# Hybrid decoder trunk on one core: down matrices of the experts issued by ScalarE

## What is computed

```python
def run_chunk(args):
    xc, e = args
    return (jax.nn.silu(xc @ w_gate[e]) * (xc @ w_up[e])) @ w_down[e]

ys = lax.map(run_chunk, (xs, chunk_exp)).reshape(n_rows, d)
out = jax.ops.segment_sum(ys * row_w[:, None].astype(ys.dtype), row_tok, num_segments=n_tok)
```

## Time and profile before

| | us |
|---|---|
| median of 3 runs | 1696.39 (1695.54 to 1699.03) |
| the profiled execution | 1697.77 |
| its span in the trace | 1696.0 |
| PE busy | 1569.4 (93%) |
| DVE busy | 581.6 (34%) |
| ACT busy | 387.6 (23%) |
| POOL busy | 87.7 (5%) |
| gate and up matmuls, L798, x2080 | 462.4 |
| down matmuls, L822, x1040 | 237.5 |
| bytes moved | 469.47 MB, mean 277 GB/s |

### The profile page before, as it was taken

One profiled execution on the slowest core, in us unless ns is written; L12 is line 12 of the kernel. 1 busy time (PEld: TensorE's weight loads), 2 busy tenths in 40 slices (PEclk: granted clock), 3 DMA queues, 4 the chain that ended last, 5 costly groups with the idle time before them and its releaser, 6 DMA issues. The chain is left out here.

```text
span 1696.0 us, 18278 instructions
## 1 busy us (share of the span) xinstructions
PE 1569.4 (93%) x6924; PEld 742.6 (44%) x6924; DVE 581.6 (34%) x1584; ACT 387.6 (23%) x788; POOL 87.7 (5%) x93
## 2 busy tenths in 40 slices
PE   7999987999999999949999999996999999999991
PEld 4444454444444443325554455554444444444340
DVE  2111245222222222255264587534422222222225
ACT  2000021111111111122243478522111111111112
POOL 0000010000000000010000000011000000000000
PEclk9999998999999999979999899997999999999996
DMA  6261227999999999964310300134999999999994
GB/s 199 74 270 53 66 81 302 426 426 426 426 426 425 426 426 426 422 203 135 99 50 1 149 2 1 35 131 174 398 426 426 425 426 426 426 426 426 425 398 168
DMA packets 107589, 469.47 MB, mean 277 GB/s; under 512 B 24288, under 2 KB 50912, under 8 KB 56544
## 3 DMA queue, kind: packets, MB, share of 16 engines
q1 hardware_dynamic: 102288, 459.74, 66.3%
q0 software_dynamic: 5200, 8.40, 1.3%
HBM read 457.62 MB, written 19.14 MB: 281 GB/s over the span
## 5 line engine op out<-in xcount | busy, mean ns | idle before, releaser
L798 PE MATMUL ps<-raw,e_xT 128*64 128x512 f32 x2080 | 462.4, 593 | 22.9 <-DMA raw<-in_expert_w_up 22.0
L798 PEld LDWEIGHTS ps<-raw,e_xT 128*64 128x64 f32 x2080 | 152.0, 137 | 321.3 <-issue 319.9
L899 DVE TENSOR_TENSOR e_sg_hid<-e_sg_hid,ps 64x512 f32<-64x512 f32 x65 | 44.3, 681 | 567.6 <-ACT e_sg_hid L845 567.6
L822 PE MATMUL ps<-raw,e_hT 128*64 128x512 f32 x1040 | 237.5, 598 | 0.0
L402 PE MATMUL ps<-c_hT,raw 128*128 128x512 f32 x384 | 165.0, 592 | 0.2 <-ACT c_hT L347 0.2
L850 ACT ACTIVATE e_ysb<-ps 64x512 f32<-64x512 f32 x130 | 77.0, 592 | 289.3 <-PE ps L822 288.5
L845 ACT ACTIVATE e_sg_hid<-ps 64x512 f32<-64x512 f32 x65 | 38.6, 593 | 399.5 <-PE ps L798 399.5
L766 PE MATMUL ps<-m_xhi,e_pick 128*128 128x512 f32 x276 | 118.7, 430 | 9.3 <-DVE e_pick L868 9.3
L822 PEld LDWEIGHTS ps<-raw,e_hT 128*64 128x64 f32 x1040 | 68.9, 136 | 122.2 <-issue 111.3
L1436 PE MATMUL ps<-a_spare,raw 128*128 128x512 f32 x256 | 113.6, 600 | 1.5 <-ACT a_spare L1143 1.5
L402 PEld LDWEIGHTS ps<-c_hT,raw 128*128 128x128 f32 x384 | 72.9, 190 | 91.7 <-issue 91.5
(11 more groups left out here) (221 smaller groups left out, 1396.0 us busy)
## 6 DMA issues: line engine op xcount, KB each, us to landing
raw<-in_expert_w_gate SPq DMA_DIRECT2D x130, 1024.0 KB, 23.9
raw<-in_expert_w_up SPq DMA_DIRECT2D x130, 1024.0 KB, 25.1
raw<-in_expert_w_down SPq DMA_DIRECT2D x130, 1024.0 KB, 24.9
raw<-in_conv_w_in SPq DMA_DIRECT2D x12, 1024.0 KB, 9.6
k_rows<-pairs_y SPq DMA_DIRECT2D x8, 1024.0 KB, 7.8
raw<-in_w_kv SPq DMA_DIRECT2D x6, 1024.0 KB, 7.1
raw<-in_conv_w_out SPq DMA_DIRECT2D x1, 4096.0 KB, 17.9
raw<-in_attn_w_in SPq DMA_DIRECT2D x4, 1024.0 KB, 5.5
```

The source lines that it names most:

```text
L798: mm = pe.matmul(ps_gu[C - C * i:2 * C - C * i, :], xT[:, q % 2, k, u * C:(u + 1) * C], ring(m, L, p)[:, kk * F:(kk + 1) * F], start=(k == ...
L822: mm = pe.matmul(ps_y[c % 2][n * C:(n + 1) * C, :], hT[:, 2 * h + kk, :], ring(m, L, p)[:, kk * D + n * 512:kk * D + (n + 1) * 512], start ...
L899: dve.tensor_tensor(hid, sg, ps_gu[0:C, :], ALU.mult).then_inc(s_hid, 1)
```

## The change

The two down pieces of a chunk are no longer issued by SP but by ACT, in ACT's own queue. SP goes on with the four gate and up pieces of each chunk. In the step of chunk c, behind the Silu, ACT issues D0 and D1 of chunk c + 2; both waits on `s_used` before them are met by then, since the Silu waits for all four gate and up pieces of chunk c. Chunks 0 and 1 have their down pieces from `prefetch`. In an overflow chunk, ACT first loads the expert's number to a register and issues the down pieces of this same chunk, ahead of its Silu. Slots, semaphores and every other engine's work stay.

```diff
+        def act_down(act, c, e):
+
+            for p in (NPIECE * c + 4, NPIECE * c + 5):
+                act.wait_ge(s_used, p - NR + 1)
+                load_piece(act, m, L, p, e)
+
         def act_step(act, c):
 
+            if c >= E:
+                act_down(act, c, act.value_load(m.ovf_e[0:1, c - E + 1:c - E + 2], min_val=0, max_val=E - 1))
             wait(act, s_used, c * NPIECE + 4)
             wait(act, s_hid, c)
             act.activation(sg, ps_gu[C:2 * C, :], ACT.Silu).then_inc(s_sg, 1)
+            if c + 2 < E:
+                act_down(act, c + 2, c + 2)
             act_rows(act, c + PAIR)
             wait(act, s_used, c * NPIECE + 6)
             wait(act, s_st[c % 2], c // 2 * 16)
```

and in SP's step of chunk c:

```diff
-                for p in range(NPIECE * c, NPIECE * (c + 1)):
+                for p in range(NPIECE * c, NPIECE * c + 4):
                     if p >= NR:
                         sp.wait_ge(s_used, p - NR + 1)
                         load_piece(sp, m, L, p, e)
```

## The result

The changed kernel takes 1718.80 us (1717.45 to 1721.79), the kernel before 1696.92 (1695.54 to 1699.03): a ratio of 1.0126, 95% interval 1.0109 to 1.0142. The forecast was 1717.4. The profiled executions lie 19.9 us apart (1697.77 and 1717.68), their spans 20.0 (1696.0 and 1716.0). The median moved 2 us more than the profiled execution did, which lies near the lower end of its kernel's runs.

A forecast was written before the change was run, and what follows sets the result against it. PE sets the pace until its head start runs out near chunk 22, then the transfers at 426 GB/s. Layer 0: 3.4 + 9.2 - 2.0 = 10.6; layer 1: 3.4 + 9.2 - 2.2 = 10.4; together +21.0, 1717.4 us, range 1703 to 1727.

The forecast's parts named there:

- Restart: Start of each expert stage: transfers resume later, as the first down pieces wait for ACT's Silu; 3.4 us lost per layer.
- Early down pieces: Expert stages: ACT's queue gets half the engines, so T(c), the landing of chunk c's U1, comes 9.2 us later per layer.
- The end: Last chunks of each layer: gate/up pieces get the engines alone, periods shrink to PE's 13.95; -2.0 and -2.2 us.
- ACT's issues: ACT between Silu and eviction of the rows: two issues of 0.80 us fit into its idle time; 0 us.
- ACT held up: Rival, ACT's issues: a full SP queue makes them wait as SP's own do; +26 to +31 us, chance 0.12.
- Overflow chunk: Layer 1's last chunk: its down pieces, issued late by ACT, are hidden by a microsecond or so; 0 us.
- terms 1 and 2: Each layer's restart, 3.4 us, and early down pieces, 9.2 us: together 12.6 us less head start for PE.
- the signs: PE's waits for U1: 43 us in about 40, first near chunk 11; periods 13.95, then 15.06; down pieces landing within 10-13 us.
- Order kept: Rival, transfer engines: both queues are served by age, so only the restart is lost; +6.9 us, 1703.3, chance 0.12.
- A faster pair of queues: Rival, transfer engines: gaps filled from the second queue raise the rate; at 440 GB/s some 7 us faster, 1689; chance 0.12.
- Later issue as the cause: Rival posed with the experiments: down pieces cost because issued later, whatever the queue; about 1718.8 us with one queue; no chance given.
- A price for each piece in the second queue: Rival posed with the experiments: each moved down piece costs its share by contention; 19/30 of 13.8 us for 19 chunks; no chance given.

The follow-up runs named there:

- e1: Against the kernel before: SP issues all pieces in its one queue, down pieces of chunk c+2 behind G0 and U0 of chunk c+3; ratio 1.0036 to the kernel before.
- e2: Against the changed kernel: SP issues the down pieces of chunk 2 at their old place; ratio 1.0099 to the kernel before.
- e5: Against the changed kernel: SP issues the down pieces of chunks 2 and 3 at their old place; ratio 1.0099 to the kernel before.
- e9: Against the changed kernel: SP issues down pieces of chunks 2 to 21 in the old order, ACT only those from chunk 22 on; ratio 1.0083 to the kernel before.
- e7: Against the changed kernel: ACT's issue moved from behind the Silu to behind the eviction of the result; ratio 1.0108 to the kernel before.
- e6: Against the changed kernel: ACT issues down pieces of chunks 4 to 21 alone, SP the others in the old order; ratio 1.0013 to the kernel before.
- e3: Against the changed kernel: ACT issues down pieces of chunks 3 to 21 alone, SP the others in the old order; ratio 1.0014 to the kernel before.
- e8: The changed kernel measured again with nothing changed; ratio 1.0120 to the kernel before.
- e4: Against the changed kernel: ACT issues D1 alone, D0 stays with SP at its old place; ratio 1.0035 to the kernel before.

## Why the prediction was right, step by step

**Restart, 3.4 us per layer.** Right in place, and in size where it stands alone: no transfers until 280, SP's gate the first issue, e1's 3.00 and 3.15. What I missed is that the next chunk's down pieces leave a gap as soon as the first is closed (e2, e5). The changed kernel has only the first gap: its transfer share is 1.02 between 293 and 294 us, so the sum did not suffer.

**Early down pieces, +9.2.** Right in kind, and in size with some luck. With the restart it made 12.6 us at T(30); the Silu of chunk 30 came 720.29 - 279.18 = 441.11 us behind the first, 12.0 later than before. In layer 1 it was 11.6. The half share is shown: 1.75 MB against 1.66 MB in the same 8 us. The landings agree: 10.9 us over all pieces of ACT, and 13.4 in the middle, just above the 10 to 13 forecast.

The luck is in what the 9.2 us stand for. A piece's landing adds 16 to its semaphore in 16 counts of 1, and PE waits for the last: wherever PE has waited, the Silu starts 3.8 us behind it, save where the clock fell. The traces keep the time of each count. For U1 of chunk 30 (times from the first Silu of the layer):

| | layer 0 | layer 1 |
|---|---|---|
| first to last count, before, us | 7.4 | 10.5 |
| first to last count, after | 11.7 | 13.6 |
| mean count later than before | 10.8 | 8.9 |
| last count later than before | 12.0 | 11.6 |
| the same in e1, mean and last | 2.8, 3.0 | 3.2, 3.2 |

With e1's restart taken off, the early pieces delay the mean count by 8.0 and 5.7 us, not by 9.2. The rest of what PE lost is that the counts lie further apart with two queues at work, and that was in no term of the prediction. e9, which has no restart, says the same: 6.9 and 5.3 us in the mean, 8.4 and 8.5 in the last count. Why they lie further apart stays open.

**The end, -2.0 and -2.2.** Right: the last period of layer 0 fell from 15.91 to 13.89, the last two of layer 1 from 30.07 to 27.96. PE in chunk 32, the last of layer 1, with no wait between the two halves of gate and up (32 matmuls in one row) or before the down matmuls:

```profile
1667.16 7.04 PE L798 MATMUL ps<-raw,e_xT 128*64 128x512 f32 x32
1677.53 3.65 PE L822 MATMUL ps<-raw,e_hT 128*64 128x512 f32 x16
```

**ACT's issues, 0.** Right. A pair takes 0.82 us and starts with the Silu, not behind its end (704.11 and 704.12 above), so even less of the gap is used; one issue has a median of 0.378 us and a maximum of 1.051. The idle time of ACT before `e_rows` is 113.3 us against 113.4 before. ACT was not held up. The changed kernel alone can't refute the rival of ACT held up by a full SP queue, since SP's issues were short in it (last section). e9 does: at its switch an issue of SP took 11.44 us, while ACT's pair beside it took 0.90 (558.00 above), and the eviction of the rows stood at 560.01, 2.02 us behind the Silu as before:

```profile
558.58 11.44 SPq L426 DMA_DIRECT2D raw<-in_expert_w_up  x1
...
560.01 0.60 ACT L839 ACTIVATE e_rows<-ps 128x512 f32<-128x512 f32 x1 [1.42 <-PE ps L766]
```

ACT's issues over the whole changed kernel (shortest, median and longest in ns):

```profile
L426 ACTq DMA_DIRECT2D raw<-in_expert_w_down x122: 334/378/1051, 279.2 to 1669.3; - x122
```

**Overflow chunk, 0.** Right, with more room than I gave it: ACT issued its two pieces at 1668.76, 0.2 us behind the eviction (I had taken 1.5 from SP), and PE did not wait.

```profile
1667.38 1.20 ACT L860 ACTIVATE e_ysb<-ps 64x512 f32<-64x512 f32 x2 [4.54 <-PE ps L822]
1668.76 0.89 ACTq L426 DMA_DIRECT2D raw<-in_expert_w_down  x2
```

**The sum.** 21.0 forecast, 19.5 in the two stages, 19.9 in the profiled execution, 21.9 in the medians. The small excess of the sum over the trace lies in terms 1 and 2, which made 12.0 and 11.6 us by chunk 30 instead of 12.6.

**What the signs got wrong.** I expected about 40 waits from chunk 11 on with even periods of 15.06. There were 30, from chunk 13 in layer 0 and 12 in layer 1, 37.8 us in all, and the periods alternated, 13.89 and 16.18 near the end. The mean is the old pace; the unevenness means that some chunks don't wait at all. The unevenness lies in the last of U1's 16 counts: for chunks 16 to 30 of layer 0 the first count comes 7.6 to 8.0 us later than before each time, the last one anything from 10.2 to 12.6. A guess was that down pieces still under way at T(c) make the next period long and the one after short. e7, which has none under way then, should have been even and was not, so why the last counts alternate stays open. The single periods over 17.7 us are another matter: they hold a stretch of lower clock (last section). The prediction had the clock at 1.00 throughout and no term for it; in the changed kernel's one case, in layer 1, the Silu again follows U1 by the usual 3.8 us before the stage ends, so the sum did not suffer.

**The rivals.** Order kept: refuted by the landing times, and e1 shows what it would have given. ACT held up: refuted by the changed kernel and e9, as said above. A faster pair of queues: refuted, 426 GB/s before and after. Later issue as the cause: refuted by e1. A price for each piece in the second queue: refuted by e6 with e9. No kernel here beats the one before; the best, e6, is 0.13% slower, by keeping the old order where it counts.

## What to carry to other kernels

Here the transfers were the bound, and a second queue added no bandwidth (426 GB/s before and after). It changed the order of arrival: each queue got its half whether its data was wanted soon or late. Ask of every piece moved to another queue which piece it overtakes, and who waits for that one. What is fetched too early is a debt: it costs nothing while the consumer still has a head start or time to catch up, and nearly all of it where the stage ends. And when one period of many is longer than the rest, read the clock of that stretch before you look for a late piece.

## What the hardware showed that I had not expected

- With its down pieces gone, SP's issues no longer took 2.10 us each as in the earlier trace rows: between 560 and 620 us each of them takes 0.33 or 0.43, although its pieces need longer to land than before (29.8 against 23.9 us over the run for gate). I read this as a full queue slowing the engine that issues into it: some eleven pieces were under way in SP's queue before, some eight after (estimates, from the times to landing and the issues per period). Where the limit lies was not measured.
- ACT issues a transfer while its activation is still running: the pair behind the Silu starts 0.01 us after the Silu does.
- PE's granted clock can fall within a stage that is otherwise full. In the expert stages of all eleven kernels 14 periods are over 17.7 us (one in the changed kernel, the others in e2, e3, e5, e6, e7, e8 and e9), and in just these 14 the granted clock is 0.50 for a stretch. The kernel before, e1 and e4 have no such stretch, and no period over 16.2. Each time PE was in, or just behind, a wait of 1.97 to 5.29 us for U1, and 16 matmuls then took 5.17 to 6.11 us instead of 3.65, with the transfers at their 426 GB/s. A long wait alone doesn't decide it: the changed kernel also has one of 3.05 us with the clock at 1.00 behind it, in a period of 17.08. Its one case, PE and the window behind:

```profile
1567.54 5.35 PE L798 MATMUL ps<-raw,e_xT 128*64 128x512 f32 x16 [2.59 <-DMA raw<-in_expert_w_up]
...
1569.00:1571.00 2.00, 2.00 (x8) 0.76 (x6) 0.00 (x0) 0.00 (x0) 0.00 (x0) 0.50 0.99 416
```
